# Interleaving 32-row and 128-row expert products in the 160-row place of a routed SwiGLU kernel

## The reference, cut to what matters

```python
# x: 256 tokens, D 1024; 8 experts, F 3584; every token uses its top 2
for e in range(8):
    out = out + combine[:, e:e+1] * (silu(x @ w_gate[e]) * (x @ w_up[e])) @ w_down[e]
```

## Time and profile before

| | |
|---|---|
| time, median of 3 runs | 1360.09 us (1359.58 to 1362.78) |
| profiled execution: its time | 1363.97 us |
| profiled execution: its span | 1362.2 us |
| TensorE busy / VectorE / ScalarE | 93% / 51% / 35% |
| HBM read | 421.2 MB |

### The profile page before, as it was taken

How to read it: one execution, slowest core, us unless ns; L and a number is a source line. 1 busy time by engine, 2 the same in 40 slices (tenths; PEclk the granted TensorE clock), 3 DMA queues, 4 the chain that set the end, 5 groups by cost and what they waited for, 6 DMA issues and landing times.

```text
span 1362.2 us, 19132 instructions
## 1 busy us (share of the span) xinstructions
PE 1268.6 (93%) x7624; PEld 788.6 (58%) x7624; DVE 689.7 (51%) x1260; ACT 470.9 (35%) x773; POOL 99.5 (7%) x115
## 2 busy tenths in 40 slices
PE   6999899999899999899899999979899999999786
PEld 5856478888785657688444333427476566533222
DVE  7997877777579667579231041114365372200002
ACT  3762444444366225467121001023355351300000
POOL 4530100000453000000000000000000000000000
PEclk9999999999999999899999999999999999999999
DMA  9533355535322387999999999999999899999995
GB/s 320 149 124 124 112 198 186 185 124 201 140 93 91 108 312 250 421 413 414 421 415 413 421 415 415 418 416 417 415 416 405 324 419 416 421 423 422 426 419 213
DMA packets 104178, 423.52 MB, mean 311 GB/s; under 512 B 19552, under 2 KB 21784, under 8 KB 95896
## 3 DMA queue, kind: packets, MB, share of 16 engines
q1 hardware_dynamic: 98904, 421.75, 78.0%
q10 hardware_dynamic: 5184, 0.52, 0.3%
HBM read 421.20 MB, written 1.05 MB: 310 GB/s over the span
## 4 chain that ended last, share of the span: by engine, by line
PE 69%; DMA 14%; DVE 12%; ACT 2%; issue 2%; SPq 1%; POOL 0%; DVEq 0%; ACTq 0%
PE psall L2830 8%; DMA m_ring<-in_moe_w_down_dram 7%; PE psall L2699 5%; PE psall L2957 5%; DMA m_ring<-in_moe_w_up_dram 4%; PE psall L2480 4%; PE psall L2797 4%; PE psall L2811 4%; PE psall L2798 4%; PE psall L2799 4%; PE psall L2851 4%; PE psall L2584 3%; PE psall L2707 3%; PE psall L3034 2%; PE psall L2762 2%; PE psall L2648 2%
## 5 line engine op out<-in xcount | busy, mean ns | idle before, releaser
L1949 DVE TENSOR_TENSOR ring_low<-m_ring,part_hi 128x896 fp32r<-128x896 f32 (+2 forms) x192 | 202.2, 1088 | 86.2 <-ACT part_hi L1447 65.5
L1447 ACT ACTIVATE part_hi<-m_ring 128x896 fp32r<-128x896 f32 (+2 forms) x192 | 177.5, 951 | 153.2 <-DMA m_ring<-in_moe_w_down_dram 69.1
L2830 PE MATMUL psall<-m_ring,xeT 128*64 128x448 f32 (+1 forms) x1280 | 200.7, 548 | 11.1 <-DMA m_ring<-in_moe_w_up_dram 7.6
L2830 PEld LDWEIGHTS psall<-m_ring,xeT 128*64 128x64 f32 (+1 forms) x1280 | 69.0, 127 | 135.0 <-issue 106.3
L2699 PE MATMUL psall<-hnT_pair,w_hi 128*128 128x512 f32 x352 | 123.6, 394 | 0.7 <-DVE hnT_pair L2096 0.7
L2308 DVE TENSOR_TENSOR hid<-e_silu,psall 128x448 f32<-128x448 f32 x28 | 17.1, 619 | 205.7 <-PE psall L2830 165.9
L2957 PE MATMUL psall<-m_ring,hidT 128*32 128x256 f32 (+1 forms) x784 | 101.7, 477 | 11.9 <-DMA m_ring<-in_moe_w_down_dram 11.2
L1899 DVE TENSOR_TENSOR w_lo<-ring,w_hi 128x1024 fp32r<-128x1024 f32 x66 | 80.2, 1222 | 43.5 <-ACT w_hi L1436 43.5
L2797 PE MATMUL psall<-part_hi,xe_hi 128*128 128x448 f32 x256 | 96.0, 375 | 1.5 <-DVE ring_low L1949 1.1
L2798 PE MATMUL psall<-part_hi,xe_lo 128*128 128x448 f32 x256 | 94.8, 370 | 0.0
L2799 PE MATMUL psall<-ring_low,xe_hi 128*128 128x448 f32 x256 | 94.7, 370 | 0.0
(11 more groups left out here) (373 smaller groups left out, 1801.0 us busy)
## 6 DMA issues: line engine op xcount, KB each, us to landing
m_ring<-in_moe_w_gate_dram SPq DMA_DIRECT2D x128, 896.0 KB, 19.7
m_ring<-in_moe_w_up_dram SPq DMA_DIRECT2D x128, 896.0 KB, 17.6
m_ring<-in_moe_w_down_dram SPq DMA_DIRECT2D x64, 1792.0 KB, 20.9
ring<-in_w_in_dram SPq DMA_DIRECT2D x10, 2048.0 KB, 13.6
ring<-in_ffn_w_gate_dram SPq DMA_DIRECT2D x5, 2048.0 KB, 11.1
ring<-in_ffn_w_up_dram SPq DMA_DIRECT2D x5, 2048.0 KB, 7.7
ring<-in_ffn_w_down_dram SPq DMA_DIRECT2D x5, 2048.0 KB, 7.9
ring<-in_w_out_dram SPq DMA_DIRECT2D x4, 2048.0 KB, 8.3
```

Of the source, the lines that this page charges most:

```text
L1447: nc.scalar.activation(part_hi[:, n % AHEAD, 0:part_cols(n)[1]], part_raw(n), ACT.Copy).then_inc(part_high, 1)
L1949: V.tensor_tensor(part_raw(n, True), part_raw(n), part_hi[:, n % AHEAD, 0:part_cols(n)[1]].bitcast(F32), ALU.subtract).then_inc(part_low, 1)
L2830: ins = M(m_bank(key)[q:q + shape[0], 0:MH], x[:, i, 0:shape[0]], w[:, m * MW + s * MH:m * MW + (s + 1) * MH], start=(i == 0), stop=(i == ...
```

## The change

In place 4 the 32-row gate and up products of one unit pair are put one pair ahead of the 128-row gate parts: pairs 0 and 1, gate parts 0 and 1, pair 2, gate parts 2 and 3, pair 3, gate parts 4 to 7, then the up parts. The planner's events follow that order. In the down products each row block of the 32-row products gets its own event, and a low part waits for the event of its own row block only. Places without a 32-row tile beside a 128-row tile keep their order.

```diff
@@ planner, gate_up
-            if 32 in shape:
-                for h in range(UH - 1):
+            def quad(h):
+                if 32 not in shape or h >= UH:
+                    return
+                if h < UH - 1:
                     self.event(("qh", it, c, h))
+                    return
                 self.add(("w", it, c), "V", self.misc())
                 for q in range(2):
                     self.quiet(("ws", it, c, q))
+
+            quad(0)
             for kind, who in (("g", "A"), ("u", "V")):
                 for i in range(KT):
+                    if kind == "g" and i % UK == 0:
+                        quad(i // UK + 1)
                     self.part((it, c, kind, i))
@@ planner, down
             if 32 in self.shape(it):
+                for r in range(MB - 1):
+                    self.event(("qd", it, c, r))
                 if len(keys) > 2:
                     self.add(keys[0], "A", keys[0][2])
-                    self.free[("qd", it, c)] = self.n
+                    self.free[("qd", it, c, MB - 1)] = self.n
                 else:
-                    self.event(("qd", it, c))
+                    self.event(("qd", it, c, MB - 1))
@@ VectorE, low
                         if kind == "d":
-                            dve.wait_ge(m_ready, experts.free[("qd", it, c)])
+                            dve.wait_ge(m_ready, experts.free[("qd", it, c, ROWS[i][0])])
@@ TensorE, gate_up
+                def quad_units(h):
+                    if 32 not in shape or h >= UH:
+                        return
+                    for kind in "gu":
+                        unit_wait(pe, it, c, kind, h, k)
+                    ins = quad(h)
+                    if h < UH - 1:
+                        event(ins)
+
                 def wide(kind):
                     for i in range(KT):
+                        if kind == "g" and i % UK == 0:
+                            quad_units(i // UK + 1)
                         n = experts.part_no[(it, c, kind, i)]
@@
                 elif shape[0] == P:
-                    if 32 in shape:
-                        for h in range(UH):
-                            for kind in "gu":
-                                unit_wait(pe, it, c, kind, h, k)
-                            ins = quad(h)
-                            if h < UH - 1:
-                                event(ins)
+                    quad_units(0)
                     for kind in "gu":
                         wide(kind)
```

## The result

The changed kernel takes 1374.91 us (median of 4 runs, 1373.87 to 1375.31) against 1361.43 us before: ratio 1.0095, 95% interval 1.0077 to 1.0113. That is 13.5 us slower. Slower was forecast, but 1366.0 with a range that ended at 1369.5, so the size was wrong. The profiled execution took 1375.18 us with a span of 1373.4, against 1363.97 and 1362.2 before.

The account below looks back on a forecast made before the run. DMA bounds the routed part except one gap, whose end compute sets. Two chunks at 3.6 us each minus 1.3 from the down edit gives +5.9, put on the median 1360.09: 1366.0 us, range 1362.3 to 1369.5.

Parts of the forecast that it names:

- The bound and where it is read: Routed part: DMA-bound except one gap losing 5.8 us; compute between 980 and 1069 sets when that gap ends.
- the issue that ends the gap: SP's load issue at 1069.09, waiting on down products of (4,1); forecast 5.9 us later, all of it on the end.
- The DMA queue has work either way: In (4,1), loads land 5.6 and 4.3 us later than an idle queue needs, so shifted releases are worth nothing.
- The stall: TensorE idles ahead of gate part 4 behind SiLU, high part and low part: 3.4 us, part 4 3.6 later.
- The drains: TensorE changing between 32-row groups and wide parts: 0.1 a group, 0.2 per chunk.
- The clock: TensorE's granted clock, put at no change in the sum; drops to half clock were kept only as rivals.
- a drop behind each stall: Rival: each new stall brings half clock, +5.9 + 3.0 = +8.9, 1369.0 us; chance 0.12.
- The rows of 906 to 918: Profile rows where TensorE idled 1.49 and 3.14 us with clock at 1.00; taken as evidence against clock drops.
- signs of being wrong: No idle before part 4; gap ending unmoved; second gap behind (4,3); granted clock differing between 980 and 1069.
- The down edit: Down products of (4,1): low part starts after its own row block, 1.3 us gained; (4,0) gains 0.
- (4,0) and (4,3): Place 4's chunks off the path: (4,0) DMA-bound, nothing; (4,3) behind the gap, nothing, 0.3 if short.
- The cover of 3.9 us: Behind (4,3), the load issued at 1137.52 lands 8.6 us later against 4.7 for an idle queue; judged just enough.

Follow-up runs that it names:

- e1: The changed kernel with the old gate and up order (all four 32-row groups first), only the down edit kept: 1359.25 us, ratio 0.9982.
- e5: The changed kernel with the new gate and up order in chunks (4,1) and (4,2) alone, down edit kept: 1371.52 us, ratio 1.0073.
- e6: The changed kernel with the new gate and up order in chunk (4,0) alone, down edit kept: 1359.46 us, ratio 0.9986.
- e8: The changed kernel with SiLU and hidden values of the 32-row products behind all eight gate parts instead of behind part 3: 1361.77 us, ratio 1.0001.
- e2: The changed kernel with every down low part waiting again for all seven row blocks, so the gate and up order alone: 1375.8 us, ratio 1.0107.
- e4: The changed kernel with six useless TensorE products behind the last 32-row group of each chunk of place 4: 1369.26 us, ratio 1.0064.
- e7: The changed kernel with the new gate and up order in chunk (4,3) alone, down edit kept: 1361.03 us, ratio 0.9999.
- e3: The changed kernel with high and low parts 4 and 5 made before the SiLU and hidden values of the 32-row products: 1365.18 us, ratio 1.0027.

## Why the prediction was right in direction and wrong in size

- **The bound and where it is read.** Right. The end follows the issue that ends the gap: in e1, e5 and e6 the rest after it is 292.9 us, before 293.1. Against the text, the gap itself did not grow: 8.2 between landings against 8.0. Everything ahead of it became late as well, and DMA lost its time in new holes behind the stalls, since the load into the slot that gate unit 2 frees goes out late. "The DMA queue has work either way" in (4,1) was wrong: the load issued at 1015.18 found it idle. That costs nothing of its own while TensorE is the bound.
- **The stall.** Right in place and cause: 3.31 us measured, 3.4 in the sum, in all four chunks; e8 removes it by order alone. The range took 4.0 per chunk as its upper bound, though the bounds worked out above it ended at 4.9; at full clock, (4,3) measured 4.1.
- **The drains.** Too small: 0.2 per chunk in the sum, 0.65 to 0.75 measured (e8, with no idle: 26.64 - 25.99 = 0.65; (4,3) of the changed kernel: 29.95 - 3.31 - 25.89 = 0.75). I counted the loss from a 32-row group into the parts but not the one on the way back: in (4,1) of the changed kernel the two pairs of parts that stand between groups take 2.67 and 2.65 us against 2.49 before. Two more groups stand alone, so there are four more changes of kind in a chunk, some 0.16 us each. The Trainium skill (TensorEngine Tiling (Array Packing), Key Properties) has a drain at each change of tiling mode; the 0.16 agrees with it, but no run separates a drain from another cost of the change.
- **The clock. This is the step that failed.** The sum set it at nothing, and kept a drop behind each stall as a rival with 0.12, priced at 1.5 per stall. The rows of 906 to 918, where 1.49 and 3.14 of idle left the clock at 1.00, were taken as evidence against it. In the profiles of the changed kernel, e2 and e5 the clock fell in all six chunks on the path, at 1.4 to 2.9 us each (31.38 to 32.81 against 29.95 with the same stall at full clock). e4 shows that it is the idle that brings it: with the wait filled, it stayed up in all four chunks. Of the signs of being wrong that the prediction names, two came: a granted clock that differs between 980 and 1069, and a second gap behind (4,3). Here the rule of the Trainium skill (TensorE: Matmul & The Clock Gate, Part 1), that activity releases the throttle, was the better guide than the one row.
- **The down edit.** Right: 1.3 forecast, 1.5 measured in the trace of e1 and of the changed kernel; (4,0) gained nothing.
- **(4,0) and (4,3).** (4,0) costs nothing, as said (e6). (4,3) was put at nothing, "and 0.3 if short"; it costs 1.8 (e7). This step failed as well. The cover of 3.9 us was held against the chunk's own 3.6; the chunk alone was 4.1 longer at full clock and 5.6 where the clock fell, and in the changed kernel it began 0.9 later behind the issue that ends the old gap, since the down products of (4,2) waited longer for a down unit and then ran at half clock. So the load that was issued at 1137.52 before, 68.4 us behind that issue, goes out 73.4 us behind it, 5.0 later, finds the queue all but idle (5.1 us to landing against 8.6) and leaves the hole at 1150. The rest of the changed kernel is 2.4 longer than before; that is more than the 1.1 by which 5.0 exceeds the cover, so the cover of that one load is not the whole price, and what makes the difference was not tried.

```profile
1100.95 3.01 PE L2931 MATMUL psall<-m_ring,hidT 128*32 128x256 f32 x32 [2.71 <-DMA m_ring<-in_moe_w_down_dram]
```

- **The sum again, with measured terms**, for the path from the profile of before: chunk (4,1) +6.8, chunk (4,2) +4.1 (its 27.48 held 1.5 of half clock already), down -1.5, makes 9.4, which is what the path grew by. With 2.4 for the rest and 0.6 by which (4,1) starts earlier in the changed kernel's profile, 11.2; the spans differ by 11.2. The medians differ by 13.5, as the profiled execution of before stands 2.5 above its median and that of the changed kernel 0.3 above. 1.5 of the 2.5 may be the half clock at 1032, which e1, e6 and e7 don't show; how often the kernel before has it was not counted, so this stays open.
- **The base** was the median of three runs, 1360.09; later it came out at 1361.2. That is 1.1 of the 8.9 by which the forecast missed. The others are the clock with 4.3 (e4), (4,3) with 2.4 and the drains of two chunks with 1.1; the stall and the down edit took back 0.4. That makes 8.5; each term is from one execution, so it could not be expected to come nearer.

## What to carry to other kernels

When work is moved ahead of other work on one engine, look at what the *other* engines have standing in their program order behind it: here the SiLU waited for the last moved group, and the next part's two preparing steps stood behind the SiLU, while the stock of four parts had been spent already. Price an idle on TensorE with the half clock that can follow it, as a term of the sum and not as an outside chance. A stall costs what it does to the one wait that sets the end; the same 3.31 us, with the extra changes of kind and the half clock behind it, cost nothing that could be measured in a DMA-bound chunk and about 6 us in one on the path.

## What the runs showed of the hardware that was not expected

The same idle of 3.31 us was followed by a fall of the clock in 9 of 12 chunks in the five profiles that have it (changed, e2, e5, e6, e7; by the chunk's length, over 31 against 29.9 to 29.95), among them all six in (4,1) and (4,2), and neither of the two (4,3) in kernels with the new order everywhere. Shorter idles were followed by one as well: the 1.11 us ahead of (4,2), which all ten profiles have, in two (before, e8), and the wait of 1.75 to 2.71 us for a down unit in the down products of (4,2), which also all ten have, in three (changed, e3, e7). What TensorE did in the stretch before differs between these places; which part of it decides was not tried. Six useless products in each chunk of place 4, 2.86 us of work each time, made the kernel 5.6 us faster.
